# Larger expert rounds with four weight buffers in both layers, and token rows gathered in quarters and turned by VectorE

## The chip, the cores and the metric

One Trainium2 chip, one of its cores. The metric is the device time of one execution in microseconds (us). Engines: TensorE (PE in the profile; PEld is its weight load), VectorE (DVE), ScalarE (ACT), GpSimd (POOL), SyncE (SP), and 16 DMA engines. SP issues the weight loads (queue q1 of the profile). GpSimd issues the indirect DMAs (queue q0).

## The reference

Two layers of a hybrid backbone over 512 latent and 256 context tokens, width 1024, all float32. Each layer has a token mixer (convolution, retention, attention), which the change leaves alone, and then a mixture of experts:

```
scores = sigmoid(h @ router_w)                       # 64 experts
_, idx = top_k(scores + router_b, 6)
w = scores[idx] / sum(scores[idx]) * 2.5
out[tok] = sum over its 6 experts e of  w_e * ((silu(h @ gate_e) * (h @ up_e)) @ down_e)   # inner width 256
         + the same block with one shared set of weights
```

Layer 0 routes 768 tokens (4608 token-expert pairs), layer 1 routes 512 (3072 pairs). One expert's weights are 1024 x 512 (gate and up) and 256 x 1024 (down) float32, 3.146 MB.

## The kernel before

**Tiling of the experts.** The pairs of one expert are cut into sub-blocks of 64 rows. A *slot* is one load of one expert's weights into one of the buffers `WB[b]`. It serves one or two sub-blocks. A *round* is a fixed pattern of slots, and a loop (`Fori`) on every engine runs it `rest` times, with one more round behind the loop. `Tour(l)` holds the pattern. Layer 0 has 4 slots of 2, 1, 2, 1 sub-blocks (6 per round), and layer 1 has 3 slots of 2, 1, 1 (4 per round) and so uses three buffers. How many rounds are run is computed on the chip from the counts of the router (`meta`). A slot or sub-block without rows is still loaded and computed, and its indices lie out of bounds, so nothing is gathered or scattered for it.

**One sub-block.** GpSimd gathers rows of tokens from `hrows` in HBM by an indirect DMA (L2067), 128 rows of 4 KB for a pair of sub-blocks, one token in a partition. TensorE transposes the pair in eight steps (L1018) into PSUM, and ScalarE (L1394) and VectorE (L1944) copy half each into `HT`. TensorE multiplies by gate and up (`gate_up`, L1035, 32 matmul instructions), ScalarE makes the silu (L1399) and VectorE the product (L1949). TensorE transposes it (L1043), VectorE copies it (L1954), TensorE multiplies by down (`down`, L1055, 8 instructions), ScalarE copies the result into `YB` (L1405), and GpSimd scatters it to `y6d` in HBM (L2072). TensorE's order is written out: gate and up of the next sub-block, the transposes of the next pair, down of this one, then the small transpose of the next.

**Weight loads.** SP fills the first slots one by one (L506 gate and up, L510 down). Slots 0 and 1 are loaded once the expert numbers are known. Before slot 2 it waits for the shared expert's products (the buffer holds its weights), for `down_kept`, and for the first gather of every pair. In the loop a slot's gate and up part is loaded again as soon as its last sub-block has passed `gate_up`, and its down part after `down`. This order, with one queue, also sets when each load starts.

**Routing arithmetic.** Between the router and the first round, VectorE computes ranks, block numbers and the row of each pair (L1802 to L1878), then for each tile of 128 tokens one-hot matrices (L1896 to L1899) which TensorE multiplies into a table (L983) of `SUBS` columns. From it VectorE makes the index table. TensorE meanwhile works on the shared expert (L676) and, in layer 0, on the next layer's modulation (L692). GpSimd then issues the first gathers and one scatter of nothing for each sub-block, which sets its semaphore.

After the last round the six results of each token are loaded (`arena<-y`), weighted and summed (L2005, L1103, L1993).

## Time and profile before

| | |
|---|---|
| median of 3 runs | 2522.56 us (2517.68 to 2527.18) |
| profiled execution | 2517.68 us, span 2517.7 us |
| TensorE busy in the span | 2306.3 us (92%) |
| VectorE, ScalarE, GpSimd busy | 871.3, 626.0, 384.8 us |
| layer 0: first gate and up to end of last down | 680.8 to 1348.9 us |
| layer 1: the same | 1880.2 to 2452.1 us |
| weight loads of the experts | 138 of 3.146 MB |
| sub-blocks computed | 196 |

The span is the time from the first to the last instruction of the profiled execution. It lies within a tenth of a microsecond of that execution's own time, and 4.9 us under the median of the three runs. The two stretches of expert rounds are 1240 us, half of the whole. Granted clock of TensorE over the span is 0.969 of full speed.

### The profile page before, as it was taken

Reading aid. Unit: us, or ns where it says so; the run is one execution under the profiler, and the core shown is the slowest. Engines: PE = TensorE matmul, PEld = TensorE weight load, DVE = VectorE, ACT = ScalarE, POOL = GpSimd, SP = SyncE. Lnnn points to the kernel's source line nnn. Section 1 sums busy time; section 2 is a strip of 40 time slices with the busy share of each in tenths; the row PEclk is TensorE's granted clock in tenths of the full one; section 3 lists DMA queues with packets and bytes.
Section 4 is the critical chain, followed back from the end, with each engine's and each line's share of the span. In section 5 each row is a group of like instructions: output and inputs, shape, how many; then the busy total and the mean of one; then the engine's idle time right before and its main releaser. Section 6 shows DMA issues by size and latency. Waiting matters only on the chain.

```text
span 2517.7 us, 37685 instructions
## 1 busy us (share of the span) xinstructions
PE 2306.3 (92%) x13690; PEld 1252.8 (50%) x13690; DVE 871.3 (35%) x1825; ACT 626.0 (25%) x1264; POOL 384.8 (15%) x624
## 2 busy tenths in 40 slices
PE   5998989989799999999999698899879999999997
PEld 1464344544555555555555563354345555555545
DVE  2295765226311111111114566663351111111116
ACT  4312344121211111111112442342211111111113
POOL 0000000000122322223321000000012222222230
PEclk8999999999899999999999899999989999999999
DMA  7511000036799999999995411000159999999976
GB/s 314 237 68 37 1 1 1 18 158 246 297 417 417 402 397 401 405 403 391 406 372 181 174 67 71 0 1 17 67 201 398 424 417 411 418 395 394 389 285 235
DMA packets 104359, 625.30 MB, mean 248 GB/s; under 512 B 22299, under 2 KB 26395, under 8 KB 59489
## 3 DMA queue, kind: packets, MB, share of 16 engines
q1 hardware_dynamic: 71536, 556.11, 55.0%
q0 software_dynamic: 31312, 63.00, 6.5%
q10 hardware_dynamic: 1440, 5.24, 0.5%
q8 instruction: 46, 0.75, 0.1%
q14 instruction: 25, 0.20, 0.0%
HBM read 607.99 MB, written 61.34 MB: 266 GB/s over the span
## 4 chain that ended last, share of the span: by engine, by line
PE 71%; DMA 15%; DVE 7%; ACT 3%; issue 2%; SPq 1%; DVEq 0%; ACTq 0%; POOLq 0%
PE psum L1035 23%; PE psum L676 18%; DMA arena<-in_experts 11%; PE psum L1055 10%; PE psum L1018 3%; PE psum L847 3%; PE psum L871 2%; DMA arena<-y 2%; PE psum L785 2%; PE psum L887 2%; PE psum L759 2%; DMA arena<-in_mod_w 2%; PE psum L1043 1%; PE psum L692 1%; DVE arena L1525 1%
## 5 line engine op out<-in xcount | busy, mean ns | idle before, releaser
L1035 PE MATMUL psum<-arena 128*64 128x256 f32 x6272 | 723.4, 383 | 27.1 <-DMA arena<-in_experts 25.1
L1035 PEld LDWEIGHTS psum<-arena 128*64 128x64 f32 x6272 | 443.2, 137 | 243.5 <-issue 31.5
L676 PE MATMUL psum<-arena 128*128 128x512 f32 (+1 forms) x1360 | 507.4, 531 | 24.5 <-ACT arena L1161 12.7
L676 PEld LDWEIGHTS psum<-arena 128*128 128x128 f32 x1360 | 260.6, 194 | 266.4 <-issue 236.1
L1055 PE MATMUL psum<-arena 128*64 128x512 f32 x1568 | 375.2, 598 | 0.9 <-ACT arena L1405 0.9
L2072 POOL DMA_INDIRECT y<-arena,SIX x196 | 196.5, 1003 | 799.4 <-ACT arena L1405 775.7
L1949 DVE TENSOR_TENSOR arena<-psum,arena 128x128 f32<-128x128 f32 x196 | 57.2, 292 | 742.5 <-ACT arena L1399 735.2
L1399 ACT ACTIVATE arena<-psum 128x128 f32<-128x128 f32 x196 | 54.4, 278 | 670.4 <-PE psum L1035 621.4
L1405 ACT ACTIVATE arena<-psum 128x512 f32<-128x512 f32 x196 | 117.0, 597 | 271.3 <-PE psum L1055 271.3
L1055 PEld LDWEIGHTS psum<-arena 128*64 128x64 f32 x1568 | 106.0, 136 | 141.4 <-issue 128.2
L1954 DVE COPY arena<-psum 128x128 f32<-128x128 f32 x196 | 57.1, 292 | 272.5 <-PE psum L1043 272.5
L2067 POOL DMA_INDIRECT arena<-hrows,GIX x103 | 109.2, 1061 | 91.3 <-issue 46.1
L2063 POOL COPY GIX<-arena 128x1 int32 (+1 forms) x103 | 20.4, 198 | 631.8 <-issue 363.3
L1018 PE MATMUL psum<-con,arena 128*128 128x128 f32 x784 | 107.9, 281 | 3.6 <-issue 1.5
L1043 PEld LDWEIGHTS psum<-con,arena 128*128 128x128 f32 x196 | 27.1, 138 | 159.8 <-issue 159.8
L847 PE MATMUL psum<-arena 96*128 96x256 f32 (+1 forms) x288 | 102.5, 474 | 3.1 <-issue 3.1
L1018 PEld LDWEIGHTS psum<-con,arena 128*128 128x128 f32 x784 | 84.5, 141 | 41.6 <-issue 40.4
L1603 DVE SCALAR_TENSOR_TENSOR arena<-arena,par 128x512 f32<-128x512 f32 (+1 forms) x180 | 103.4, 649 | 0.0
L1317 ACT ACTIVATE arena<-psum,nm 128x768 f32<-128x768 f32 (+1 forms) x80 | 65.3, 816 | 111.2 <-DVE nm L1708 111.2
L2046 POOL COPY arena<-arena 32x4608 f32<-32x4608 f32 x2 | 8.0, 4019 | 538.1 <-PE psum L785 538.1
L1944 DVE COPY arena<-psum 128x512 f32<-128x512 f32 x98 | 67.9, 693 | 50.2 <-PE psum L1018 49.8
L1394 ACT ACTIVATE arena<-psum 128x512 f32<-128x512 f32 x98 | 58.5, 597 | 85.5 <-PE psum L1018 84.7
(253 smaller groups left out, 1922.6 us busy)
## 6 DMA issues: line engine op xcount, KB each, us to landing
arena<-in_experts SPq DMA_DIRECT2D x138, 2048.0 KB
arena<-in_experts SPq DMA_DIRECT2D x138, 1024.0 KB, 10.3
arena<-in_mod_w SPq DMA_DIRECT2D x48, 1024.0 KB, 19.3
arena<-y SPq DMA_DIRECT2D x20, 1536.0 KB, 16.4
arena<-in_wblk SPq DMA_DIRECT2D x22, 1024.0 KB, 4.8
arena<-in_shared SPq DMA_DIRECT2D x2, 3072.0 KB, 10.1
hrows<-arena ACTq DMA_DIRECT2D x10, 512.0 KB, 6.2
y<-arena,SIX POOLq DMA_INDIRECT x196, 6.8
```

The lines of the kernel that those rows point to most:

```text
L676: last = mm(job(l, key, n, parts), a, b, start=i == 0, stop=i == len(pairs) - 1)
L847: last = mm(flat[:, u % 2, i * LAT:i * LAT + n], QALL[0:QK, h, qt * P:(qt + 1) * P], KALL[0:QK, h, a:a + n], start=True, stop=True)
L1018: last = nc.tensor.transpose(psum[:, 5 + k // 4, (k % 4) * P:(k % 4 + 1) * P], HROW[:, p, k * P:(k + 1) * P], ident)
L1035: last = mm(psum[j * ROWS:(j + 1) * ROWS, s % 2, 0:2 * P], HT[:, s // 2, k, h:h + ROWS], w[:, k * 512 + j * 256:k * 512 + (j + 1) * 256], ...
L1055: last = mm(psum[q * ROWS:(q + 1) * ROWS, 3 + s % 2, :], AT[:, s % 2, j * ROWS:(j + 1) * ROWS], w[:, 4096 + j * D + q * 512:4096 + j * D + ...
L1317: f(PR[:, u % 2, 0:n], flat[:, u % 2, 0:n], ACT.Exp, bias=nm[:, u % 4:u % 4 + 1], scale=QK ** -0.5, accum_out=rsum[:, g % 2, place:place + ...
L1394: f(HT[:, p, 0:4, :], psum[:, 5, :].rearrange("p (k c) -> p k c", k=4), ACT.Copy).then_inc(sem(f"ht_a{l}"), 1)
L1405: f(YB[:, s, :], psum[:, 3 + s % 2, :], ACT.Copy).then_inc(sem(f"y_a{l}"), 1)
L1603: op = V.scalar_tensor_tensor(dst, src, w, dst, ALU.mult, ALU.add)
L1944: V.tensor_copy(HT[:, p, 4:8, :], psum[:, 6, :].rearrange("p (k c) -> p k c", k=4)).then_inc(sem(f"ht_d{l}"), 1)
L2067: g.indirect_dma_start(HROW[:, p, :], None, hrows[l], offsets(GIX[:, p, 3:4]), bounds_check=T * P - 1, oob_is_err=False).then_inc(sem(f"ga ...
L2072: g.indirect_dma_start(y6d[l], offsets(SIX[:, s, 1:2]), rows, None, bounds_check=TOPK * STRIDE * 2 - 1, oob_is_err=False).then_inc(sem(f"s ...
```

## The change

`Tour` gets new patterns. Both layers now have 8 slots per round over four buffers (slot b uses buffer b modulo 4), of 3, 1, 2, 1, 2, 1, 2, 1 sub-blocks in layer 0 (13 per round) and 3, 1, 1, 1, 2, 1, 1, 1 in layer 1 (11 per round). An expert's sub-blocks are cut into as many threes as go, then a two or a one. Rows are gathered one sub-block at a time, as 256 quarter rows of 1 KB by two indirect DMAs, from a copy of the tokens stored so that VectorE's 32 x 32 block transpose (`turn`) yields `HT` directly. TensorE's eight transposes and the two copies behind them go. Gathers are issued five sub-blocks ahead, through a ring of 6 or 5 row buffers. Each gather reads its place in the index table from `DQ`, which GpSimd computes itself. The results go through a ring of 4 or 5 `YB` buffers. PSUM tiles of the last sub-block of a round are their own. The routing arithmetic on VectorE is rewritten and shorter, TensorE's three counting products become one group (`rank`), and a table of 136 columns takes the place of one of 224. The wait for the first gathers ahead of slot 2 is gone. The scatters of nothing move to the start of each layer.

```diff
-SUBS = 224
+SUBS = 136
+        sizes = ((3, 1, 2, 1, 2, 1, 2, 1), (3, 1, 1, 1, 2, 1, 1, 1))[l]
...
@@ SP
-                for b in range(tour.slots):
+                for b in range(4):
                     if b == 2:
                         ready(sp, l, ("su", 1, pl.sq[-1]))
                         sp.wait_ge(sem("down_kept"), l + 1)
-                        for p in range(tour.pairs):
-                            sp.wait_ge(sem(f"gath{p}_{l}"), 16)
...
+                with sp.Fori(0, rest) as i:
+                    refills(i, range(8))
+                refills(rest, range(4))
@@ PE
-                    if s % 2 == 0:
-                        pe.wait_ge(sem(f"ht_a{l}"), i * tour.pairs + (s // 2 + 1))
-                        pe.wait_ge(sem(f"ht_d{l}"), i * tour.pairs + (s // 2 + 1))
+                    pe.wait_ge(sem(f"turned{l}"), i * n + (s + 1 + turned0))
...
-                            if ahead % 2 and not (last_round and p == 0):
-                                gather_transposed(p, i + 1 if p == 0 else i)
...
+                    elif st == "ix":
+                        for q in range(4):
+                            for fb in range(4):
+                                mm(psum[32 * fb:32 * fb + 32, pl.bank[st], q * w:(q + 1) * w], ident[:, 32 * q:32 * q + 32], TF, ...)
+                        for h in range(2):
+                            for q in range(2):
+                                last = mm(psum[q * ROWS:(q + 1) * ROWS, pl.bank[st], (4 + h) * w:(5 + h) * w], ..., TF, ...)
@@ DVE
+                def turn(s, i):
+                    r, u = tour.place(s, tour.rows_ring)
+                    dve.wait_ge(sem(f"gath{r}_{l}"), i * 32 * tour.uses(r, tour.rows_ring) + (32 * u + 32))
+                    V.transpose(HT[:, tour.third(s), :, :].rearrange("p k (t c) -> p t k c", t=2), GR[:, r, :])
...
                     for s in range(n):
                         ahead = (s + 1) % n
+                        if not (last_round and s + 2 >= n):
+                            turn((s + 2) % n, i + 1 if s + 2 >= n else i)
+                        if not (last_round and ahead == 0):
+                            hidden(ahead, i * n + (s + 1))
+                            hidden_in(ahead, i * n + (s + 1))
@@ POOL
+                def gather(s, i):
+                    d = pool.value_load(DQ[0:1, tour.order[s], column(...)], min_val=0, max_val=EMPTY)
+                    g.tensor_copy(IX[:, s, 0:3], IXT[:, bass.ds(d, 1), :])
+                    pool.wait_ge(sem(f"ix{l}"), i * n + (s + 1))
+                    for h in range(2):
+                        g.indirect_dma_start(GR[:, r, h * 256:(h + 1) * 256], None, rows, offsets(IX[:, s, h:h + 1]), ...)
...
+                    for s in range(n):
+                        x = s + 5
+                        if not (last_round and x >= n):
+                            pool.wait_ge(sem(f"turned{l}"), ...)
+                            pool.wait_ge(sem(f"scat{y}_{l}"), ...)
+                            gather(x % n, i + 1 if x >= n else i)
+                        scatter(s, i)
```

## Rows read from the trace of the kernel before

**Rows 1.** Chain that ended last, layer 0 (start us, us, what):
```profile
680.81 5.31 PE psum L1035 x32
...
718.63 3.60 PE psum L1035 x32
722.23 1.72 PE psum L1055 x8
724.21 3.60 PE psum L1035 x32
727.81 1.02 PE psum L1018 x8
...
730.96 3.60 PE psum L1035 x32
```
**Rows 2.** The same chain in layer 1:
```profile
2040.92 16.39 DMA arena<-in_experts
...
2067.18 15.81 DMA arena<-in_experts
```
**Rows 3.** Busy time by stretch (A:B, us, engines, granted clock, DMA share, GB/s):
```profile
718.00:1310.00 592.00, 592.00 (x4322) 317.18 (x4320) 89.26 (x240) 112.63 (x240) 175.47 (x288) 1.00 0.98 400
1960.00:2430.00 470.00, 444.15 (x3225) 247.08 (x3223) 66.35 (x178) 83.78 (x179) 131.61 (x216) 1.00 1.00 406
```
**Rows 4.** DMA queue q0 (packets, MB, share): whole span, 700 to 1300, 1960 to 2420:
```profile
q0 software_dynamic: 31312, 63.00, 6.5%
q0 software_dynamic: 14867, 35.25, 15.0%
q0 software_dynamic: 10692, 19.87, 11.3%
```
**Rows 5.** Chain at the ends of layer 0's and layer 1's rounds:
```profile
1346.93 1.95 PE psum L1055 x8
...
2450.16 1.95 PE psum L1055 x8
```
**Rows 6.** SP's DMA issues in order of time, around the first loads of both layers:
```profile
673.59 0.34 SPq L506 DMA_DIRECT2D arena<-in_experts  x1
...
1850.15 0.33 SPq L506 DMA_DIRECT2D arena<-in_experts  x1
...
1877.37 0.33 SPq L506 DMA_DIRECT2D arena<-in_experts  x1
```
**Rows 7.** GpSimd in order of time (start us, us, line, operation, [idle before]):
```profile
997.77 0.20 POOL L2063 COPY GIX<-arena 128x1 int32 x1
998.85 1.06 POOL L2067 DMA_INDIRECT arena<-hrows,GIX  x1 [0.88 <-issue]
...
1003.53 1.02 POOL L2072 DMA_INDIRECT y<-arena,SIX  x1 [3.43 <-ACT arena L1405]
1004.56 0.20 POOL L2094 COPY SIX<-arena 128x1 int32 x1
...
1871.18 1.03 POOL L2067 DMA_INDIRECT arena<-hrows,GIX  x1 [0.88 <-POOL GIX L2063]
```
**Rows 8.** Lines L2093 (near 1003), L556 and L2067: sequencer steps, then landing times:
```profile
L2093 POOLq EVENT_SEMAPHORE  x1: 17/17/17, 1003.3 to 1003.3; - x1
...
L556 SPq TENSOR_LOAD <-eids x57: 263/271/623, 1910.4 to 2390.8; - x57
...
DMA to landing us min/median/max: 2.2/10.8/11.5
```
**Rows 9.** VectorE in order of time: a table step, and a copy of 128 x 512:
```profile
1848.83 0.85 DVE L1897 TENSOR_TENSOR arena<-con,LOHI 128x672 f32<-128x672 f32 x1
...
1000.20 0.69 DVE L1944 COPY arena<-psum 128x512 f32<-128x512 f32 x1 [0.41 <-PE psum L1018]
```
**Rows 10.** TensorE in order of time, start of layer 1's rounds:
```profile
1867.05 9.56 PE L676 MATMUL psum<-arena 128*128 128x512 f32 x16
...
1880.20 3.67 PE L1035 MATMUL psum<-arena 128*64 128x256 f32 x32 [0.98 <-DVE arena L1944]
```

More of the change, by code:

```diff
@@ L73, in __init__, with third, place, uses @@
     def __init__(self, l):
-        self.ones, self.rounds = ((1, 2), (2, 1))[l]
-        self.per = 2 + self.ones
-        self.slots = self.rounds * (1 + self.ones)
-        self.subs = self.rounds * self.per
-        self.most = (34, 48)[l]
-        self.pairs = self.subs // 2
-        self.slot_of, self.kind = [], []
-        for u in range(self.rounds):
-            for k in range(1 + self.ones):
-                self.slot_of += [len(self.kind)] * (1 if k else 2)
-                self.kind.append((u, k))
+        sizes = ((3, 1, 2, 1, 2, 1, 2, 1), (3, 1, 1, 1, 2, 1, 1, 1))[l]
+        self.slots = len(sizes)
+        self.twos, self.ones = sizes.count(2), sizes.count(1)
+        self.subs = sum(sizes)
+        self.most = (36, 25)[l]
+        self.slot_of = [b for b, n in enumerate(sizes) for _ in range(n)]
+        self.order = [o for n in sizes for o in range(n)]
+        self.kind = [(n, sizes[:b].count(n)) for b, n in enumerate(sizes)]
+        self.rows_ring = (6, 5)[l]
+        self.y_ring = (4, 5)[l]
     def opens(self, s):
-        return s == 0 or self.slot_of[s] != self.slot_of[s - 1]
+        return self.order[s] == 0
     def last_sub(self, slot):
         return max(s for s in range(self.subs) if self.slot_of[s] == slot)
+    def third(self, s):
+        return 2 if s == self.subs - 1 else s % 2
+    def place(self, s, m):
+        return (m, 0) if s == self.subs - 1 else (s % m, s // m)
+    def uses(self, r, m):
+        return 1 if r == m else (self.subs - 1) // m
+    def apart(self, s, m):
+        r = self.place(s, m)[0]
+        return min((s - x) % self.subs or self.subs for x in range(self.subs) if self.place(x, m)[0] == r)
+    def block(self, b, i, rest):
+        n, m = self.kind[b]
+        if n == 3:
+            return i
+        if n == 2:
+            return rest + i * self.twos + (m + 1)
+        return rest * (1 + self.twos) + i * self.ones + (m + 1 + self.twos)
 class Plan:
@@ L198, in __init__ @@
         tiles(2)
-        self.shared += ["cum", "sum", "cnt", ("sg", 1, 0)]
+        self.shared += ["rank", ("sg", 1, 0)]
         tiles(1)
-        self.shared += ["start", "eid"]
+        self.shared += ["eid"]
         if l == 0:
@@ L576, in _, with refills @@
                     load_parameters(l + 1)
-                with sp.Fori(0, rest) as i:
-                    experts = [None] * tour.slots
+                def refills(i, bs):
+                    experts = {}
                     def refill_down(b):
@@ L977, in _ @@
+                        last.then_inc(done, 1)
                     elif st[0] == "oh" or st == "tab":
@@ L1808, in _ @@
-                evacuated(dve, l, "cnt")
-                for t in range(1, T):
-                    link(V.tensor_tensor(SUMS[:, t, :], SUMS[:, t, :], SUMS[:, t - 1, :], ALU.add))
-                tour = tours[l]
-                S1, U = tour.ones, tour.rounds
-                for q, up in enumerate((P // 2 - 1, P - 1)):
-                    V.tensor_scalar(CNTI[:, q, :], SUMS[:, T - 1, :], float(up), None, ALU.add)
-                    last = V.tensor_scalar(coli[:, q:q + 1], col[:, 0:1], float(up), None, ALU.add)
@@ L2046, in _ @@
                 g.tensor_copy(KALL[64:96, 2:HEADS, :], CAT[0:ROPE, 7:8, :].to_broadcast([ROPE, HEADS - 2, TOK])
-                              ).then_inc(sem(f"qk_ready{l}"), 1)
+                              ).then_inc(sem("qk_ready"), 1)
                 tour = tours[l]
-                n, pairs = tour.subs, tour.pairs
+                n = tour.subs
+                pool.wait_ge(sem("blocks"), l + 1)
+                iota = c("iota", 1)
+                threes, twos = (CUM[0:1, q, EXPERTS - 1:EXPERTS] for q in range(2))
@@ L2106 @@
+                            pool.sem_inc(sem("passed"), 1)
+                            gather(x % n, i + 1 if x >= n else i)
+                        scatter(s, i)
+                for s in range(5):
+                    gather(s, 0)
+                with pool.Fori(0, rest) as i:
+                    expert_round(i, False)
+                expert_round(rest, True)
 _OUT = (P, KC, LAT)
```

447 lines of the change are left out of this document (212 added, 235 removed).

## The prediction

> **What bounds the kernel now.** I read the chain that ended last first, then the busy times by stretch, then the two queues of GpSimd and SP in order of time. In layer 0 the chain runs on TensorE alone: gate and up of a sub-block begin at 718.63, 724.21 and 730.96 [rows 1], so a sub-block takes 5.58 us and every second one 6.75 us, because eight transposes of the next pair stand between (1.17 us). A round of six is 37.0 us. In layer 1 the chain is different: a load of 16 us, then sub-blocks, then a load again. Two loads of the first slot are 2040.92 and 2067.18 [rows 2], so a round is 26.3 us, where TensorE alone would need 2 x 5.58 + 2 x 6.75 = 24.7 us. The stretches confirm it. In layer 1 TensorE is busy for 444 of 470 us, and the DMA engines have a share of 1.00 at 406 GB/s. In layer 0 TensorE is busy for all of the 592 us, and the DMA engines stand at 0.98 and 400 GB/s [rows 3]. So layer 1 is bound by the DMA engines, and layer 0 by TensorE with the DMA engines 2% behind it. Whatever is taken from TensorE in layer 0 uncovers the DMA engines at once. I take 406 GB/s, the rate at a share of 1.00, as what they can do.
>
> **How many rounds.** The counts of the router decide this. I evaluated the reference's router on its own inputs and counted rows per expert: layer 0 has 15 to 170, layer 1 has 6 to 179. By the old rule that gives 18 rounds of 4 slots and 22 of 3, that is 138 loads and 108 + 88 = 196 sub-blocks, the counts that the page shows. By the new rule layer 0 has 6 threes, 25 twos and 33 ones, layer 1 has 2, 11 and 51. Both are 64 slots, and a round has 8. The twos fit too (31 with the threes in 4 x 8 places, 13 in 2 x 8). So both layers run 8 rounds: 104 sub-blocks and 64 loads in layer 0 (108 and 72 before), 88 and 64 in layer 1 (88 and 66).
>
> **TensorE's side.** Layer 0 takes 668.1 us from the first gate and up to the end of the last down, 680.8 to 1348.9 [rows 1, 5]. Four sub-blocks go (4 x 5.58 = 22.3 us) and 53 groups of transposes (53 x 1.17 = 62.0 us). The new time is 584 us. In layer 1 it would be 88 x 5.58 = 491 us, far under what the loads need.
>
> **The DMA engines' side.** Each pair moves a row of 4 KB in and one out. Layer 0: 64 x 3.146 = 201.3 MB of weights and 4608 x 8192 B = 37.7 MB of rows. Layer 1: 201.3 and 25.2 MB. The first loads lie ahead of the stream. In layer 0 the second slot's load goes out at 673.59, in layer 1 the third slot's at 1877.37 with two slots already in [rows 6]. So 63 loads and the rows (235.9 MB, 581 us at 406 GB/s) are left in layer 0, 62 and the rows (220.2 MB, 542 us) in layer 1.
>
> The trace has no quarter rows of 1 KB, so their price is bounded from both sides. The whole span's 31312 packets of q0 [rows 4] come out exactly as 103 gathers x 128, 206 scatters x 64 and 309 DMAs x 16 for their semaphores. A scatter has 128 pieces of 2 KB, so two pieces count as one packet of 4 KB. If four quarter rows share a packet too, the gathers cost nothing more (0). If each 1 KB piece is a packet of its own, I need the cost of a small packet. From the two stretches of q0 (35.25 MB are 8606 packets of 4 KB, which leaves 6261 small ones, in 15.0% of 16 x 600 us; 19.87 MB are 4851 and leave 5841, in 11.3% of 16 x 460 us [rows 4]) I get 161 ns for 4 KB and 9 ns for a small one. Some 18000 more small ones per layer, quarter rows and indices out of bounds, are 10 us over 16 engines. I take 5 us per layer, between the two, since the pairing of scatters speaks for sharing. The upper bound is that a 1 KB piece costs what a 2 KB one does (81 ns): 46 us in layer 0 and 31 us in layer 1.
> By the Trainium skill (DMA: Bandwidth & Descriptors, "Why small descriptors are slow (HBM only)") each packet has a fixed overhead of about three cycles beside 32 B per cycle. Estimated from that page, 1 KB pieces need 35/32 where 4 KB need 131/128, 7% more on the gathers' 31.5 MB, or about 5 us in both layers together. No run here shows it yet.
>
> **Starts and ends.** In layer 0 the first gate and up waits for TensorE's own list (shared expert and modulation), and the transposes and the copy behind it (2.9 us) go. The table step adds 40 small matmuls (some 2 us), and shorter routing arithmetic gives 2 to 5 us back. I take 677 for the first gate and up (681 before) and 672 for the second load. In layer 1 the stretch ahead of the rounds is a chain of VectorE. Its block arithmetic of 32 operations shrinks by some 6 us net of the weights that now stand behind it, and the wide table operations of 0.85 us on 672 elements [rows 9] have 408, which is 0.6 us less for each of 4 tiles. The table step gives 2 us of it back. The last shared product begins at 1867.05 and the first gate and up at 1880.20 [rows 10]. I take 1872 for the latter and 1870.5 for the third load. Behind the last load come 5.5 us: the last gate and up (3.6) overlaps the landing of the last down part (1 MB, 2.6 us), then two downs (1.72 + 1.95) and the small steps.
>
> **The wait that goes.** The loads of slots 2 and 3 wait for the last shared product, and in layer 1 that ends at 1876.6 (1867.05 + 9.56 [rows 10]), with the load out at 1877.37. The second and last of the two gathers went out at 1871.18 [rows 7] and takes 2.2 us from issue to landing on idle engines [rows 8]. Both had landed, so the wait costs nothing now. Its cover would be gone in the new kernel, whose first five gathers are spread over some 16 us. Without the wait the loads go out at once, and the gathers of the third to fifth sub-block then land in 10.8 us [rows 8] instead of 2.2. TensorE may stand for 2 or 3 us there in layer 1, which the loads hide.
>
> **GpSimd and VectorE.** These are the new risks, since every sub-block now has two gathers, a scatter, a copy and a register load. Rows 7 give 0.20 for the copy, 0.88 until a gather that waits for it, 1.06 per gather and 1.02 per scatter. After the scatter at 1003.53 the copy follows with no gap, and its sequencer steps stand at 1003.3, ahead of the scatter's start [rows 7, 8]. So the sequencer runs ahead, and only a wait exposes the 0.88 us. A register load takes 0.27 to 0.62 us on SP [rows 8] and lies beside the scatter. The sum is 0.20 + 0.88 + 2 x 1.06 + 1.02 = 4.2 us per sub-block, under 5.58, so it is hidden. VectorE gains a transpose of 128 x 512, for which I take the copy's 0.69 us [rows 9], and loses that copy for each pair. It runs while TensorE is in gate and up (3.6 us), and gathers are five sub-blocks (28 us) ahead of a landing of 10.8 us. Both cost nothing. ScalarE loses work.
>
> **Sum.** Layer 0: the loads end at 672 + 581 + 5 = 1258, the last down at 1263.5. TensorE by itself ends at 677 + 584 = 1261. The two are equal within their errors, and they feed each other through four buffers, so I add 4 us: 1267.5, against 1348.9, 81.4 us less. Layer 1: 1870.5 + 2 (the first slot is free only after three sub-blocks) + 542 + 5 + 5.5 = 2425, against 2452.1 (2450.16 + 1.95 [rows 5]), 27 us less. Together 108.4 us: 2517.7 becomes 2409.3. The median of the runs stands 4.9 us over the profiled execution, so I forecast 2414 us.
>
> **The rivals.**
> *GpSimd becomes the bound (the slower side).* If each of its steps pays its own start, a sub-block costs 0.55 + 0.20 + 3 x 0.88 + 2 x 1.06 + 1.02 = 6.5 us. That is 676 us in layer 0 and 572 in layer 1, about the time of now (2525 us). If in addition each new VectorE transpose holds up GpSimd for its 0.69 us, it is 7.2 us: layer 0 ends at 677 + 749 + 8 = 1434 (+85), layer 1 at 1872 + 634 + 8 = 2514 (+62), together about 2670 us. It decides from 6.4 us per sub-block on, where layer 0 (668/104) has its old time. Against it speak the missing gap and the sequencer ahead [rows 7, 8]. For it speaks that no two indirect DMAs stand directly behind each other in the loop of now.
> The Trainium skill (SBUF — State Buffer, "Who interferes with whom") says that a VectorE operation in a two-port mode, or with two SBUF inputs, and a GpSimd operation lock each other out for a whole instruction. By that rule the transpose from SBUF to SBUF may add its time to GpSimd's 4.2 us, 4.9 us, still under 5.58; alone it changes nothing.
> *Quarter rows are dear.* At the upper bound both layers are bound by the loads and take 41 and 26 us more than forecast: 2481 us. For it speaks that nothing of 1 KB is in the trace, against it that q0's bytes cost only 5 to 7% more engine time than q1's.
> *The engines can do more.* Stretches of 420 GB/s and more occur. At 425 GB/s layer 0 falls to TensorE's 1261 and layer 1 ends 24 us sooner: about 2384 us.
> *The change doesn't do what it says.* If the counts gave a ninth round in layer 0 (three experts more over 64 rows would do it), 13 x 5.58 = 72.5 us come back: 2487 us.
>
> **How the numbers follow.** Forecast (2395 to 2440) 0.60, dear quarter rows or more interplay of loads and TensorE (2440 to 2495) 0.17, more DMA rate (2375 to 2395) 0.10, ninth round 0.03, GpSimd at 6.5 us (about 2525) 0.04, GpSimd at 7.2 us 0.06. The range that holds 8 in 10 is 2382 to 2475. It leaves out the far end of the dear rows, the ninth round, GpSimd and a little at the bottom. A measurement of this kernel can tell about 0.5% (12.6 us) from no change. Faster by more than that is 0.89, within it 0.04, slower 0.07.
>
> **What would show it.** Right: no transposes between gate and up and down, starts 5.58 us apart in layer 0, 64 loads per layer, a DMA share of 0.99 to 1.00 in both layers at 400 to 410 GB/s, loads ending near 1258 and 2420, GpSimd idle before each scatter. Wrong: GpSimd with no idle time before its scatters, VectorE's transposes waiting for gathers, a lower GB/s at a share of 1.00 (dear pieces), or gaps of TensorE behind a load in layer 0 while the DMA share is under 0.95, which would be the ring of four running dry.

## The result and the profile after

The changed kernel takes 2408.55 us (median of 4 runs, 2402.2 to 2412.91), the kernel before beside it 2521.32 us. The ratio is 0.9546, 95% interval 0.9521 to 0.957. The forecast was 2414 us, so it was 5 us high. The profiled execution took 2402.2 us, and its span is 2400.4 us, against 2517.7 us. The mean granted clock is 0.966 (0.969 before).

The lines of the page that the change touches (busy us, mean ns of one, idle time before them and what ended it), then the two DMA queues (packets, MB, share of the span):

```profile
PE 2174.2 (91%) x12802; PEld 1173.2 (49%) x12802; DVE 910.6 (38%) x1858; ACT 566.3 (24%) x1170; POOL 674.1 (28%) x811
...
L1056 PE MATMUL psum<-arena 128*64 128x256 f32 x6144 | 715.5, 386 | 39.2 <-DMA arena<-in_experts 31.2
...
L2085 POOL DMA_INDIRECT arena<-hrows,IX x384 | 394.1, 1026 | 228.1 <-POOL IX L2081 163.1
...
L2093 POOL DMA_INDIRECT y<-arena,IX x192 | 197.1, 1027 | 305.7 <-DVE arena L1929 146.2
...
L1929 DVE STREAM_TRANSPOSE arena<-arena 128x512 f32<-128x512 f32 x192 | 135.8, 707 | 124.6 <-DMA arena<-hrows,IX 121.8
...
arena<-in_experts SPq DMA_DIRECT2D x128, 2048.0 KB, 20.9
```
```profile
q1 hardware_dynamic: 68656, 524.73, 54.1%
q0 software_dynamic: 34672, 63.07, 7.0%
```

There are 128 loads, 192 sub-blocks (6144 matmuls of gate and up, 32 each) and 384 gathers. Those are eight rounds in both layers. TensorE has 132 us less to do and GpSimd 289 us more. The transposes of TensorE are gone, and VectorE has 192 of 0.71 us.

The chain that ended last, layer 0 (start us, us, what), answers to [rows 1, 5]:

```profile
672.85 5.38 PE psum L1056 x32
...
696.16 3.60 PE psum L1056 x32
699.76 1.72 PE psum L1078 x8
701.48 0.26 PE psum L1064
701.74 3.60 PE psum L1056 x32
...
1164.86 26.11 DMA arena<-in_experts
...
1255.16 1.95 PE psum L1078 x8
```

From the second one on, gate and up begin 5.58 us apart, and nothing but TensorE stands between them. The first distance is 6.50 us, and one is 6.10 us: there the one load of the layer that is on the chain stands, and TensorE waited 0.30 us for it. So layer 0 is TensorE's 584.3 us, from 672.8 to 1257.1. Its last load had landed at 1249.3. In layer 1 the chain consists of loads again, as in [rows 2]:

```profile
1841.56 20.56 DMA arena<-in_experts
...
1864.45 3.63 PE psum L1056 x32
...
1868.31 21.02 DMA arena<-in_experts
...
2334.69 1.95 PE psum L1078 x8
```

The busy times by stretch (columns as in [rows 3]) show both layers at the DMA engines' limit:

```profile
710.00:1150.00 440.00, 440.00 (x3235) 230.33 (x3233) 100.11 (x236) 69.11 (x158) 258.03 (x315) 1.00 1.01 413
1850.00:2300.00 450.00, 409.84 (x2938) 223.14 (x2936) 87.48 (x216) 62.99 (x144) 234.60 (x286) 0.98 1.01 411
```

At a share of 1.01 they move 413 GB/s in layer 0 and 411 in layer 1, and the share of 1.00 before was 406. In layer 0 TensorE and the DMA engines are both full, and TensorE's end is the later one.

Where the 117.3 us of the two spans lie (a layer counts from its first gate and up to the end of its last down; "between" ends at layer 1's first gate and up; all us):

| | start | layer 0 | between | layer 1 | behind | span |
|---|---|---|---|---|---|---|
| before | 680.8 | 668.1 | 531.3 | 571.9 | 65.6 | 2517.7 |
| after | 672.8 | 584.3 | 529.8 | 549.8 | 63.8 | 2400.4 |
| difference | -8.0 | -83.8 | -1.6 | -22.1 | -1.8 | -117.3 |

The -1.6 us hides two parts. From layer 1's router (its first product on TensorE, at 1805.54 before and 1719.24 after) to the first gate and up it is 7.0 us shorter. That is the shorter routing arithmetic together with the transposes and copies that no longer stand ahead of the first gate and up, and no run separates the two. From the end of layer 0 to the router it is 5.5 us longer, and the longer part is the combination of the results (below).

### The profile page after: what moved, and what is told of

It is laid out like the page before. It is cut to its first block, busy times and chain, and to the rows that moved or that the text cites. A ratio compares the mean times of both kernels' runs of the same rounds, so it can differ in the third digit from the quotient of the medians.

```text
span 2400.4 us, 36613 instructions
## 1 busy us (share of the span) xinstructions
PE 2174.2 (91%) x12802; PEld 1173.2 (49%) x12802; DVE 910.6 (38%) x1858; ACT 566.3 (24%) x1170; POOL 674.1 (28%) x811
## 3 DMA queue, kind: packets, MB, share of 16 engines
q0 software_dynamic: 34672, 63.07, 7.0%
## 4 chain that ended last, share of the span: by engine, by line
PE 68%; DMA 18%; DVE 7%; ACT 3%; issue 2%; SPq 1%; POOL 0%; POOLq 0%; DVEq 0%; ACTq 0%
PE psum L1056 22%; PE psum L704 18%; DMA arena<-in_experts 13%; PE psum L1078 10%; PE psum L875 3%; PE psum L899 2%; DMA arena<-y 2%; PE psum L915 2%; DMA arena<-in_mod_w 2%; PE psum L787 2%; PE psum L813 2%; PE psum L1064 1%; DVE arena L1544 1%; PE psum L720 1%; PE psum L1122 1%
## 5 line engine op out<-in xcount | busy, mean ns | idle before, releaser
L1056 PE MATMUL psum<-arena 128*64 128x256 f32 x6144 | 715.5, 386 | 39.2 <-DMA arena<-in_experts 31.2
L2085 POOL DMA_INDIRECT arena<-hrows,IX x384 | 394.1, 1026 | 228.1 <-POOL IX L2081 163.1
L1078 PE MATMUL psum<-arena 128*64 128x512 f32 x1536 | 363.5, 593 | 6.9 <-DMA arena<-in_experts 5.7
L2093 POOL DMA_INDIRECT y<-arena,IX x192 | 197.1, 1027 | 305.7 <-DVE arena L1929 146.2
L1936 DVE TENSOR_TENSOR arena<-psum,arena 128x128 f32<-128x128 f32 x192 | 55.9, 291 | 503.9 <-ACT arena L1420 503.9
L1428 ACT ACTIVATE arena<-psum 128x512 f32<-128x512 f32 x192 | 114.7, 597 | 310.7 <-PE psum L1078 310.7
L1929 DVE STREAM_TRANSPOSE arena<-arena 128x512 f32<-128x512 f32 x192 | 135.8, 707 | 124.6 <-DMA arena<-hrows,IX 121.8
L1064 PEld LDWEIGHTS psum<-con,arena 128*128 128x128 f32 x192 | 26.5, 138 | 160.0 <-issue 160.0
L1726 DVE TENSOR_REDUCE mx<-psum 128x1 f32<-128x768 f32 (+1 forms) x80 | 67.9, 849 | 32.0 <-PE psum L875 30.8
L1122 PE MATMUL psum<-con,arena 128*128 128x128 f32 x480 | 62.6, 295 | 18.7 <-DVE arena L1991 11.3
L915 PE MATMUL psum<-con,arena 128*128 128x128 f32 x416 | 61.7, 280 | 18.6 <-ACT arena L1357 10.0
```

Source lines behind the costliest of these rows:

```text
L915: last = nc.tensor.transpose(psum[:, bk, at * P:(at + 1) * P], PR[:, u % 2, i * P:(i + 1) * P], ident)
L1056: last = mm(psum[j * ROWS:(j + 1) * ROWS, (0, 1, 5)[u], 0:2 * P], HT[:, u, k, :], w[:, k * 512 + j * 256:k * 512 + (j + 1) * 256], start=k ...
L1078: last = mm(psum[q * ROWS:(q + 1) * ROWS, (3, 4, 6)[u], :], AT[:, u, j * ROWS:(j + 1) * ROWS], w[:, 4096 + j * D + q * 512:4096 + j * D + ...
L1122: last = mm(job(l, ("ct", t, i))[:, k * P:(k + 1) * P], Y6[:, t % 3, y, m * P:(m + 1) * P], ident, start=y == 0, stop=y == 2)
L1428: f(YB[:, r, :], psum[:, (3, 4, 6)[tour.third(s)], :], ACT.Copy).then_inc(sem(f"y_a{l}"), 1)
L1726: link(V.reduce_max(mx[:, q], flat[:, u % 2, 0:n], AX))
```

## Experiments: what bounds each layer

My theory: layer 0 is bound by TensorE with the DMA engines close behind, layer 1 by the DMA engines, and the number of rounds sets both. Four edits move one side each. All are edits of the changed kernel, each executed once. The six kernels of this document that leave layer 0's rounds as they are took 584.3 to 584.9 us there, so 1 us counts in layer 0. Layer 1 also depends on how its start falls (last experiments below), so a few us there say little.

**TensorE's transposes put back** (without the copies behind them):

```diff
                             gate_up(ahead, j)
+                            if ahead % 2:
+                                for k in range(8):
+                                    nc.tensor.transpose(psum[:, 7, (k % 4) * P:(k % 4 + 1) * P], ident, ident)
```

> The new kernel with TensorE's old extra work put back and nothing else: eight 128 x 128 transposes of a constant into an unused PSUM bank after gate and up of every second sub-block (1.17 us each time in the old kernel). Theory (layer 0 bound by TensorE, layer 1 by the weight loads): layer 0 longer by 52 x 1.17 = 61 us, layer 1 by 0 to 8 us (TensorE would need 491 + 44 x 1.17 = 542 us of some 550), together 2462 to 2478 us. Rival (layer 0 is bound by the loads too): layer 0 longer by under 50 us, together under 2455 us.

Measured: 2471.12 us. Layer 0 took 639.9 us (+55.6), layer 1 555.0 (+5.3). The expectation had 52 and 44 groups. The condition holds for six sub-blocks of 13 and five of 11 per round, so the added line runs 704 times in 88 groups, 48 in layer 0 and 40 in layer 1. That is 55.6 / 48 = 1.16 us for one group in layer 0, the 1.17 us that the prediction read from [rows 1]. The 40 groups in layer 1, 47 us of TensorE's time, cost 5.3 us, since TensorE waits for loads there anyway.

**Half of the bytes of the down part in the loop's loads left out:**

```diff
+            def load_down(l, b, e, n=WEXP - WGU):
+                sp.dma_start(WB[b][:, WGU:WGU + n], A["experts"][bass.ds(e + l * EXPERTS, 1), :, WGU:WGU + n].rearrange(
...
-                        load_down(l, b % 4, experts[b])
+                        load_down(l, b % 4, experts[b], 1024)
```

The down product then uses weights of an earlier expert for half of its columns, so this kernel computes other results.

> The new kernel, but in the loop and the last round the down part of an expert brings only half its columns (0.524 MB less per slot, so the down product uses stale weights there). Theory: layer 0 stays within 3 us, since TensorE bounds it. Layer 1 falls from about 550 us to TensorE's 88 x 5.58 = 491 us, together about 2350 us. Rival (layer 0 is load-bound too): layer 0 shorter by 20 us and more. Rival (layer 1 is bound by TensorE or by the latency of its ring, not by bytes): layer 1 within 10 us of before, 2400 us.

Measured: 2347.7 us. Layer 0 583.4 (-0.8), layer 1 495.8 (-54.0), which is near the 491 us that the prediction gave TensorE alone. The DMA share fell to 0.91 at 357 GB/s in layer 0, and its time stayed. So layer 0's time is TensorE's, and layer 1's is the loads'.

**Half a MB more per load in the loop**, from the experts' weights into a spare piece of HBM, each copy after the one before it has landed:

```diff
+                sp.sem_inc(sem(f"extra{l}"), 16)
...
+                        sp.wait_ge(sem(f"extra{l}"), i * 128 + (16 * b + 16))
+                        sp.dma_start(spare, A["experts"][bass.ds(experts[b] + l * EXPERTS, 1), :, WGU:WGU + 1024].rearrange("o p n -> (o p) n")).then_inc(sem(f"extra{l}"), 16)
                         load_down(l, b % 4, experts[b])
```

> The new kernel with an extra copy of 0.524 MB from the expert weights to a spare place in HBM for every slot that is loaded again (60 per layer, 31.5 MB per layer), on SP's queue ahead of the down part. Theory (the DMA engines are within a few per cent of TensorE in layer 0): layer 0 goes from 584 to (235.9 + 31.5) / 412 = 649 us, layer 1 from 550 by 31.5 / 411 = 77 us, together about 2550 us. Rival (the DMA engines have 10% and more to spare in layer 0, their share of 1.0 notwithstanding): layer 0 longer by under 20 us, together under 2510 us.

Measured: 2554.7 us. Layer 0 660.1 (+75.8), layer 1 626.2 (+76.4).

```profile
720.00:1200.00 480.00, 438.11 (x3095) 227.66 (x3092) 91.01 (x225) 65.75 (x151) 246.71 (x303) 0.96 0.99 406
```

TensorE is now idle in layer 0 too (busy for 438 of 480 us), and the engines move 406 GB/s. The 31.5 MB are 77.5 us at that rate, so both layers paid about the full price. The expectation had only 65 us for layer 0: its loads were taken to need 573 us of 584 at 412 GB/s, and the 11 us of reserve were to come off. That reserve does not show. At 406 GB/s all bytes of this run take 659 us, which is what layer 0 took. Why the engines moved 406 GB/s here and 413 without the copies is open. The copies go from HBM to HBM and wait for each other, which the loads do not. Taking bytes away brought layer 0 nothing, adding them cost the full price: it sits on the edge between the two.

**A ninth round in both layers**, with empty slots:

```diff
-                V.tensor_scalar(meta[0:1, 0:1], tot[0:1, 0:1], 2.0, 1.0, ALU.max, ALU.subtract)
+                V.tensor_scalar(meta[0:1, 0:1], tot[0:1, 0:1], 9.0, 1.0, ALU.max, ALU.subtract)
```

> The new kernel made to run nine rounds in each layer instead of eight (the result is the same, the ninth is empty). Theory: layer 0 longer by 13 x 5.58 = 72.5 us, layer 1 by eight loads of 3.146 MB at 411 GB/s = 61 us (TensorE's 61.4 us in that round is the same), together about 2542 us. Rival (the number of rounds matters little, what was gained came from the steps inside a round): under 60 us more in all.

Measured: 2543.19 us. Layer 0 658.3 (+74.0, and 13 x 5.58 = 72.5 by the prediction), layer 1 615.0 (+65.2). So one round more would have taken back most of what layer 0 gained, and the other steps rest on the count of rounds.

## Experiments: GpSimd's margin

The steps of GpSimd for one sub-block near the start of layer 0 (start us, us, line, operation, [idle before]):

```profile
699.91 1.05 POOL L2085 DMA_INDIRECT arena<-hrows,IX  x1 [0.85 <-POOL IX L2081]
701.26 1.00 POOL L2085 DMA_INDIRECT arena<-hrows,IX  x1 [0.30 <-issue]
703.12 1.03 POOL L2093 DMA_INDIRECT y<-arena,IX  x1 [0.86 <-DVE arena L1929]
704.16 0.19 POOL L2081 COPY IX<-arena 128x3 int32 x1
```

By their sum a sub-block takes 0.19 + 0.85 + 1.05 + 0.30 + 1.00 + 0.30 + 1.03 = 4.7 us of 5.58. The prediction had 4.2, since it set nothing between two indirect DMAs that follow each other. How much is there before it counts? One more operation of one partition was put ahead of the copy, once without a wait and once with a wait of the copy for it (each executed once):

```diff
+                    g.tensor_scalar(scr[:, :], iota, 3.0, None, ALU.mult)
                     g.tensor_copy(IX[:, s, 0:3], IXT[:, bass.ds(d, 1), :].rearrange("p o w -> p (o w)"))
```

> The new kernel with one more GpSimd operation per sub-block (a scalar multiply of 1 x 288 into a spare tile, 1.0 us in the trace) ahead of the index copy. From the new trace GpSimd's steps are 0.20 + 0.85 + 1.05 + 0.30 + 1.01 + 0.30 + 1.03 = 4.74 us when nothing is waited for. Theory: 5.74 us is over TensorE's 5.58, so layer 0 grows by 104 x 0.16 = 17 us, layer 1 (6.25 us per sub-block) not, together about 2426 us. Rival (the 4.2 us of the prediction): 5.2 us still fits, no change.

```diff
+                    g.tensor_scalar(scr[:, :], iota, 3.0, None, ALU.mult).then_inc(sem(f"ix{l}"), 1)
+                    pool.wait_ge(sem(f"ix{l}"), i * 2 * n + (2 * s + 1))
                     g.tensor_copy(IX[:, s, 0:3], IXT[:, bass.ds(d, 1), :].rearrange("p o w -> p (o w)"))
-                    pool.wait_ge(sem(f"ix{l}"), i * n + (s + 1))
+                    pool.wait_ge(sem(f"ix{l}"), i * 2 * n + (2 * s + 2))
```

> The same, but the index copy waits for the added operation, which exposes another 0.88 us. Theory: 4.74 + 1.0 + 0.88 = 6.6 us per sub-block, layer 0 longer by 104 x 1.04 = 108 us, layer 1 by 88 x 6.6 - 550 = 31 us, together about 2548 us. Rival (4.2 us): 6.1 us per sub-block, layer 0 longer by 54 us, layer 1 not, about 2462 us.

Measured without the wait: 2413.99 us, layer 0 593.9 (+9.6), layer 1 551.3 (+1.6). With it: 2435.95 us, layer 0 613.7 (+29.4), layer 1 551.8 (+2.0). GpSimd without the wait, then two lines of the one with it:

```profile
1000.94 1.11 POOL L2088 DMA_INDIRECT arena<-hrows,IX  x1 [0.85 <-POOL IX L2084]
1002.35 1.01 POOL L2088 DMA_INDIRECT arena<-hrows,IX  x1 [0.30 <-issue]
1003.66 1.04 POOL L2096 DMA_INDIRECT y<-arena,IX  x1 [0.30 <-issue]
1004.74 0.94 POOL L2083 TENSOR_SCALAR scr<-con 1x288 f32<-1x288 f32 x1
```
```profile
1005.49 0.18 POOL L2084 COPY IX<-arena 128x3 int32 x1 [0.18 <-POOL scr L2082]
1006.53 1.12 POOL L2088 DMA_INDIRECT arena<-hrows,IX  x1 [0.86 <-POOL IX L2084]
```

Now nearly no scatter waits for data. The one shown has [0.30 <-issue] ahead of it, and 6 of layer 0's 104 stand idle for more than 0.4 us, where it was 100 of 104 in the changed kernel. So GpSimd sets the pace. Its cycle is 1006.67 - 1000.94 = 5.73 us, and 1006.53 - 1000.58 = 5.95 us with the wait. Over 104 sub-blocks that is (5.73 - 5.58) x 104 = 16 us and (5.95 - 5.58) x 104 = 38 us. Measured were 9.6 and 29.4, 6 and 9 us less. The lead of the gathers covers the rest. In the changed kernel layer 0 ends 26.5 us after its last sub-block's gathers begin (1230.6 to 1257.1), and in the two runs 19.0 and 16.9 us after (1249.5 to 1268.5, 1270.6 to 1287.5). So GpSimd fell behind by 16 and 38 us and used up 7.5 and 9.6 us of lead doing so. The expectation of the second run was far too high, because I had put the 0.88 us of [rows 7] on every wait. A copy that waits pays 0.18 us. The 0.85 us belong to an indirect DMA that waits for its indices.

So the rival in which GpSimd becomes the bound is real and some 0.9 us per sub-block away, and above that edge it costs what the cycle exceeds 5.58 us by, less the lead: an operation of 0.94 us cost 9.6 us of 2400. Layer 1, where the loads are the bound, took 1.6 and 2.0 us more, which is within what its start varies by.

## Experiments: the combination of the results

TensorE and ScalarE in the stage behind layer 0, changed kernel:

```profile
1314.42 7.33 PE L1122 MATMUL psum<-con,arena 128*128 128x128 f32 x48 [7.35 <-DVE arena L1979]
```
```profile
1322.17 2.71 ACT L1465 ACTIVATE arena<-arena 128x512 f32<-128x512 f32 x5 [6.20 <-PE psum L1113]
```

And the same TensorE step in the kernel before:

```profile
1404.84 2.94 PE L1103 MATMUL psum<-con,arena 128*128 128x128 f32 x24 [1.12 <-DVE arena L2005]
```

Before, TensorE made a tile as soon as VectorE had it (1.1 us idle time). Now it stands for 7.35 us and then makes two. The code gives PSUM banks in turn over all jobs, and two tiles of this stage (`ct(4, *)` and `ct(5, *)`) have banks written out as numbers. The shared list lost jobs to the `rank` group, the turn starts elsewhere, and the written bank of `ct(4, 0)` is now that of `ct(3, 1)`, which must be read out first. The edit sets the turn back where it was:

```diff
+            if l == 0 and i == self.before_experts:
+                bk, turn = 4, 5
             if l == 0 and k[0] == "ct" and k[1] >= 4:
```

> The new kernel with the PSUM banks of layer 0's last products (shared down and the sums of six results) numbered as in the old kernel, so that the fifth tile's first half does not lie in the bank of the fourth tile's second half. Theory (the combine stage of layer 0 became 5.5 us longer by that collision): 5.5 us shorter, about 2403 us, and TensorE no longer waits 7 us for VectorE before the fifth tile. Rival (it is the initial scatters that moved there, or chance): no difference.

Measured: 2399.1 us (median of 4 runs, 2395.48 to 2401.54), ratio to the kernel before 0.9517 [0.949, 0.9543]. The waits are gone (start us, us, TensorE, same stage):

```profile
1308.16 2.95 PE L1124 MATMUL psum<-con,arena 128*128 128x128 f32 x24 [1.49 <-DVE arena L1993]
1312.24 2.95 PE L1124 MATMUL psum<-con,arena 128*128 128x128 f32 x24 [1.13 <-DVE arena L1993]
```

The traces of all kernels show the same. From the end of layer 0's rounds to the end of the last of these products on TensorE it is 74.9 us in the kernel before and 80.4 us in the changed one. The nine kernels without the bank edit (the changed one and eight edits of it) take 78.7 to 80.4 us, and the three with it 72.9 to 73.3 us. So the collision costs some 6 us, and the edit takes it away. "Between" is 524.3 us instead of 529.8 here, but in the seven other kernels that have neither the bank edit nor the early product it lies from 526.3 to 531.9 us, so that one difference alone would say little. The medians alone would not prove it either, since the intervals of the two ratios overlap. This version is clearly faster than the kernel before. Its four runs all lie under the four of the changed kernel, by 9.4 us in the medians. That is more than the 5.5 us expected. Counted from the same point, its layer 1 also ended 1.4 us sooner, by a chance that the next section shows, and the rest is open.

## Experiments: the loads that are not held, and layer 1's start

TensorE in order of time at layer 1's start, then VectorE, then a piece of the chain:

```profile
1786.86 3.67 PE L1056 MATMUL psum<-arena 128*64 128x256 f32 x32 [1.69 <-DVE arena L1929]
1794.82 0.30 PE L1064 MATMUL psum<-con,arena 128*128 128x128 f32 x1 [4.29 <-DVE arena L1936]
```
```profile
1793.79 0.71 DVE L1929 STREAM_TRANSPOSE arena<-arena 128x512 f32<-128x512 f32 x1 [7.03 <-DMA arena<-hrows,IX]
...
1794.42 0.25 DVE L1936 TENSOR_TENSOR arena<-psum,arena 128x128 f32<-128x128 f32 x1
```
```profile
1785.63 8.03 DMA arena<-hrows,IX
```

The third and fourth loads, 6 MB that SP issues one behind the other, are called the flood below. The third goes out at 1786.04, 0.4 us after the gather of the second sub-block. The rows of that gather take 8.0 us to land instead of 2.2 [rows 8]. VectorE stands 7.0 us in its transpose, and the product of the first sub-block (L1936), which TensorE needs, is behind that transpose in VectorE's order. TensorE is idle for 4.3 us, and the granted clock is 0.66 on the mean from 1795 to 1800, so the second gate and up runs partly at the lower of the clock's two levels (1.2 and 2.4 GHz). Is this what the missing wait costs? The wait put back, for the first two sub-blocks' rows:

```diff
                         sp.wait_ge(sem("down_kept"), l + 1)
+                        for r in range(2):
+                            sp.wait_ge(sem(f"gath{r}_{l}"), 32)
```

> The new kernel with the wait put back: SP holds the loads of slots 2 and 3 until the rows of the first two sub-blocks have landed, in both layers. Theory (layer 1 is bound by the loads from the start): in layer 1 gate and up of the second sub-block comes 4 us sooner, but the third load 2 to 3 us later, and the end of the rounds is 2 to 3 us later; layer 0 does not change, its rows land 15 us before. Rival (the 4 us in which TensorE stands at the start of layer 1 count): 4 us shorter.

Measured: 2404.71 us (2402.68 to 2409.11), ratio 0.9547 [0.9521, 0.9574], the same as without it. Both effects are there and cancel. The second gate and up came 3.5 us sooner relative to the first, and the third load went out at 1790.16, 3.4 us later relative to the same. The rows of the third sub-block then met the flood (7.61 us to land), and layer 1 took 549.7 us where it was 549.8.

The other way would be to start the loads sooner still. They wait for the shared expert's last product, which in layer 1 stands behind the table. The edit moves it ahead of the table, as in layer 0, and SP then waits for the table instead:

```diff
-        if l == 0:
-            self.shared.append(("su", 1, 0))
+        self.shared.append(("su", 1, 0))
...
-                        ready(sp, l, ("su", 1, pl.sq[-1]))
+                        ready(sp, l, "tab" if l else ("su", 1, 1))
...
-                    if t == 2 and l == 0:
+                    if t == 2:
                         shared_hidden(1, 0)
...
-                if l:
-                    shared_hidden(1, 0)
```

> The new kernel with layer 1's last shared product (16 matmuls, 7.9 us, which stood between the index table and the first expert) computed before the tiles are transposed, as layer 0 does; SP then waits for the table instead before it loads slots 2 and 3. Theory (layer 1 is load-bound, so what counts is when the third load goes out): the third load 8 us sooner, the end of layer 1's rounds 6 to 9 us sooner. Rival (the chain of VectorE, or the row stores, take the place of the product): under 2 us.

> Both edits together, the banks and the early shared product. Theory: they lie in different stages, so the gains add to 12 to 14 us against the new kernel, about 2395 us, ratio to the old kernel 0.949. Rival: the bank order of the early product gives part of it back.

Measured with the early product alone: 2407.76 us, ratio 0.9556 [0.9527, 0.9584]. With the bank edit as well 2406.04 us, ratio 0.9544 [0.9522, 0.9566], so no gain is left of it. Both theories failed. The third load went out at 1782.87, only 3.2 us sooner, the table step ended later, and the first gate and up began at 1794.14, 7.3 us later. The first gather went out at 1785.14, behind the four issues of the two loads, and its second half, at 1786.58, landed after 6.60 us. Then the first gate and up was slow itself:

```profile
1794.14 6.01 PE L1053 MATMUL psum<-arena 128*64 128x256 f32 x32 [12.45 <-DVE arena L1924]
```

It took 6.01 us for the 3.67 of the changed kernel at 1786.86. The granted clock was 0.50, the lower level, from 1780 to 1795, and 0.60 during this step. TensorE had just stood idle for 12.45 us. In the changed kernel the shared product of 7.9 us stood directly ahead of this point, the clock rose during it, and it was 1.00 at the first gate and up. So moving the product also cost 2.3 us of clock. The other two kernels with the early product pay the same (5.02 us at 0.72 and 6.06 us at 0.60), and the ones without it do not. No run separates the missing product from the longer idle time.

The rest of the loss is in the DMA engines (busy time by stretch of the early kernel, columns as in [rows 3]):

```profile
1790.00:1795.00 5.00, 0.86 (x4) 0.59 (x6) 0.71 (x1) 0.00 (x0) 3.38 (x5) 0.50 1.04 430
1795.00:1800.00 5.00, 5.00 (x30) 3.05 (x26) 0.71 (x1) 0.00 (x0) 3.23 (x4) 0.61 0.99 397
1800.00:1805.00 5.00, 4.17 (x37) 3.11 (x37) 1.29 (x3) 0.28 (x2) 3.22 (x4) 1.00 0.59 216
1805.00:1810.00 5.00, 5.00 (x39) 2.61 (x37) 1.20 (x3) 0.87 (x2) 1.23 (x2) 1.00 0.04 9
1810.00:1815.00 5.00, 5.00 (x39) 2.56 (x37) 1.20 (x3) 0.87 (x2) 3.15 (x4) 1.00 0.80 283
```

The two loads had landed by about 1803, and the next one needs a free slot, that is three sub-blocks of TensorE's work. It went out at 1810.80. The engines stood for 5 x (0.41 + 0.96 + 0.20) = 7.9 us. Loads that go out sooner only lengthen this hole if TensorE does not start sooner too.

The last run puts the two together, to see whether it is the flood that holds the first rows: bank edit, early product, and the wait of the run with the wait.

> The bank edit and the early product of the run before, and in addition the third and fourth loads wait until the first two sub-blocks' rows have landed. If it is the flood of loads that holds up the first rows once the shared product no longer covers them (theory), these rows now land in 2 to 3 us instead of 6.6, the third load goes out near 1788 instead of 1783 (on the clock of the run with the early product alone) and the first gate and up of layer 1 begins near 1789 to 1790 instead of 1794; the whole is 2398 to 2404 us, level with the bank edit alone or 4 us under the version with both edits and no wait. If it is VectorE's late transposes and the late table step that hold up the start (rival), the first gate and up stays at 1793 to 1795 with the wait, the third load is 4 to 5 us later as well, and the whole comes to 2406 to 2411 us.

Measured: 2403.55 us (2398.2 to 2410.51), ratio 0.9537 [0.9516, 0.9558]. The second half of the first rows landed in 2.90 us instead of 6.6, so the flood was the cause of that part:

```profile
1775.97 2.90 DMA arena<-hrows,IX
```

To compare the starts I count from the step on ScalarE that gives the expert numbers of layer 1 (L1400 in the changed kernel), since the stages ahead differ by up to 9 us:

| from there, us | table step | first gate and up | third load | end of layer 1 | third load to end |
|---|---|---|---|---|---|
| changed | 25.3 | 36.6 | 35.8 | 586.4 | 550.6 |
| bank edit | 25.3 | 38.1 | 37.3 | 585.0 | 547.7 |
| with the wait | 25.3 | 36.5 | 39.1 | 586.3 | 547.1 |
| early product | 29.7 | 44.0 | 32.7 | 591.4 | 558.7 |
| early, bank edit | 28.7 | 42.9 | 31.7 | 588.9 | 557.2 |
| early, bank edit, wait | 27.3 | 37.8 | 41.4 | 588.5 | 547.1 |

The end of layer 1 moves by 6 us in all. It is the third load's start plus 547 us where the DMA engines have no hole, and 3 to 12 us more where they have one (in the changed kernel the reload of the first slot goes out at 1806.37, with a share of 0.73 from 1805 to 1810). The bank edit alone has no hole although it holds nothing: its third load goes out 1.5 us later from the same point, the second gate and up begins 4.8 us after the first instead of 8.3, and the stall of TensorE is gone. So 1.5 us decide whether the flood meets the second sub-block's rows. These 1.5 us are luck and no work of the edit. The flood waits for the shared product, and that product took 9.41 us at a granted clock of 0.76 with the bank edit, and 7.91 us at 0.90 in the changed kernel: the clock rose later there. So the 1.4 us by which layer 1 ends sooner (585.0 against 586.4) are a chance of the clock. Without the hold the loads start sooner and wait longer, with it they start later and run through. On the whole time the last run is inconclusive: its median is at the edge of the theory's range, and its runs spread over both ranges. On the first gate and up the theory held (37.8 us instead of 42.9). The third load was later than both had it, since it waits for the gathers of two sub-blocks, and the last of these went out 37.4 us after the expert numbers, 2 us later than in the changed kernel.

## Why the prediction was right, point by point

- **Eight rounds in both layers**: as said, 64 loads each and 104 and 88 sub-blocks.
- **TensorE's side of layer 0**: 584 us forecast, 584.3 measured, and the run with transposes gave 1.16 us per group for the 1.17 read from [rows 1].
- **The DMA rate** was a mis-sized term: 406 GB/s, the rate at a share of 1.00 in [rows 3]. Measured 411 and 413, at a share of 1.01, which is about half of that difference. Layer 0's loads alone would then take 235.9 / 0.412 = 573 us instead of 581, so they ended ahead of TensorE (the last load had landed at 1249.3, where I had 1258), and of the 4 us for interplay 0.3 us were on the chain. With the loads' bound of 1263.5 and these 4 us gone, layer 0's rounds gave 83.8 us, where I had 77.4.
- **Layer 0's start**: 672.8, where I had 677. In the other runs of this document, which have the same program ahead of it, it lies from 671.9 to 678.1. So a profile cannot tell this term better than by some 5 us, and half of my miss may be that.
- **Quarter rows**: 5 us per layer forecast. q0's 34672 packets are exactly 384 x 32 for the gathers, 203 x 64 for the scatters and 587 x 16 for DMAs' semaphores. So four pieces of 1 KB share one packet of 4 KB, the lower end of my bounds. By the single packets of the trace, q0 took 164.2 us of each of the 16 engines before and 167.7 us after, 3.5 us more for both layers together, where I had 10. A packet of 4 KB in q0 took 161.9 ns on the mean before and 162.6 ns after, so all of the increase is in smaller packets. The page of the Trainium skill that I weighed against it (DMA: Bandwidth & Descriptors, "Why small descriptors are slow (HBM only)") puts a fixed overhead on each packet, and my estimate of 5 us from it took each 1 KB piece as a packet of its own. The trace has no such packets, so it neither bears out that estimate nor contradicts the page, and that 5 and 3.5 us are near each other is chance.
- **Layer 1**: 27 us less forecast up to the end of its rounds, 29.2 measured from the router on. Two misses stand against each other in this. The third load to the end takes 550.6 us, where I had 554.5, and the third load went out 5.0 us sooner after the router than before, where I had 6.9.
- **The wait that goes** costs nothing before, and in the new kernel TensorE stands for it, as I said. I had 2 to 3 us at the third to fifth sub-block. It was 4.3 us at the second, because VectorE's transpose of the next stands ahead of the product of this one. The gather ahead of the flood was not ahead enough: 0.4 us before the third load. The run with the wait has the same time.
- **GpSimd**: 4.2 us per sub-block forecast, 4.7 measured, still hidden. The 0.30 us between two indirect DMAs were missing. The prediction weighed a rule of the Trainium skill (SBUF — State Buffer, "Who interferes with whom") by which the transpose might add its time to GpSimd's. The rule is for VectorE's two-port modes and for two SBUF inputs. The transpose has one input, and no run shows its mode, so the case is no test of the rule. What it shows is no lockout: the 57 gathers and scatters that ran beside a transpose for 0.2 us or more took 1.03 us on the mean, as did those beside none.
- **The lead of the gathers** was wrong in the prediction, and it cost nothing by a small margin. I had 28 us from a gather to its use and 10.8 us to land. In layer 0 gate and up begins 17.4 us (median) after the second gather of its sub-block, since a gather goes out behind the scatter of six sub-blocks before, and these rows take 13.0 us (median, up to 15.3) to land. VectorE did wait for rows: 79 idle times before a transpose, 121.8 us together, ended with a gather's landing. That was one of my signs of being wrong. TensorE waited for a transpose only 5 times, 6.4 us in all, so the time does not show it.
- **What no step had**: the 5.5 us of the combination (shown by the run with the banks set back). I counted what the jobs of the router cost, and not that their number sets the banks of the jobs behind them. The diff held all that was needed to see it.

The sum was 108.4 us and the spans differ by 117.3. The misses are 6.4 (rounds of layer 0), 4.0 (its start), 2.2 (layer 1) and 1.8 us (behind the rounds), against 5.5 us (combination). The median of the changed kernel stands 8.2 us over its span, and I had 4.9, which took back 3 us of the rest. So the mechanism was as forecast, and that the number was met within 5.5 us is partly luck, because errors of both signs met.

## What to carry to other kernels

Where two resources are within 2% of each other, give each its own end and take the later. Here work added to TensorE cost layer 0 its full size (55.6 us), and so did bytes added to its loads (75.8 us), while bytes taken away brought nothing (0.8 us). Whether taking work from TensorE alone would bring anything was not run. If jobs share a resource that is dealt out in turn (a bank, a buffer, a slot), removing one job moves all behind it, and a number written out by hand beside the turn is where it will collide. Starting loads sooner gains nothing while the reload of the first buffer waits for work that starts no sooner: look for a hole in the DMA share behind the first loads before moving them. Before you move work away from in front of a stage, look at the granted clock there: here the moved product had been what TensorE did while its clock rose.

## What the runs showed of the hardware

- Two indirect DMAs that follow each other on GpSimd have 0.30 us between them (1.00 to 1.05 us each). One that waits for its indices starts 0.85 us after they are written, while a copy that waits for an operation starts after 0.18 us.
- An indirect gather of 1 KB pieces made packets of 4 KB, four pieces in each, by the exact count of the packets. The 4 KB packets of q0, gathers and scatters together, took 162.6 ns each (161.9 before).
- A DMA share near 1.00 stood for rates from 400 to 413 GB/s: 400 at 0.98 and 406 at 1.00 before, 411 to 413 at 1.01 after, 406 to 410 at 0.99 to 1.00 with half a MB more per load. Part of that is the share itself. The rate divided by the share is 406 to 407 before and 409 to 410 after.
- At the start of layer 1 TensorE's clock stood at the lower level (granted 0.50) with the table's small products and an idle time of 8.7 to 12.5 us ahead of it, and 32 matmuls of gate and up took 5.0 to 6.1 us. With a product of 7.9 us directly ahead they took 3.67 us at 1.00.
- VectorE's transpose of 128 x 512 float32 in blocks of 32 x 32, SBUF to SBUF, takes 0.71 us. The copy of that shape from PSUM took 0.69 [rows 9].
